# The layer boundary of a fused eight-layer block: both norms from gathered sums, residual, scaling and split by chunks

## What is computed

```python
def rmsnorm(x, g):
    y = xf * lax.rsqrt(jnp.mean(xf * xf, axis=-1, keepdims=True) + EPS)
    return (y * g.astype(jnp.float32)).astype(x.dtype)

def modulated_sublayer(x, mod, g_pre, g_post, fn, weight):
    shift, scale, gate = mod[:, 0], mod[:, 1], mod[:, 2]
    h = rmsnorm(x, g_pre) * (1.0 + scale) + shift
    y = rmsnorm(fn(h), g_post)
    return x + weight * (1.0 + gate) * y
```

## Time and profile before

| | |
|---|---|
| time, median of 3 runs | 3411.46 us (3410.39 to 3413.81) |
| the profiled execution | 3409.45 us, its span 3407.7 us |
| PE busy | 3114.9 us, 91% of the span |
| DVE, ACT, POOL busy | 1680.2, 1172.0, 610.4 us |
| mean granted clock of PE | 0.945 of full speed |

### The profile page before, as it was taken

One profiled execution on the slowest core, in us unless ns is written; L12 is line 12 of the kernel. 1 busy time (PEld: TensorE's weight loads), 2 busy tenths in 40 slices (PEclk: granted clock), 3 DMA queues, 4 the chain that ended last, 5 costly groups with the idle time before them and its releaser, 6 DMA issues.

```text
span 3407.7 us, 39522 instructions
## 1 busy us (share of the span) xinstructions
PE 3114.9 (91%) x13788; PEld 2440.5 (72%) x13788; DVE 1680.2 (49%) x2588; ACT 1172.0 (34%) x2027; POOL 610.4 (18%) x359
## 2 busy tenths in 40 slices
PE   5999968999899997588899997997899999969999
PEld 3888846888678885376588885775777767757777
DVE  5554466554554335786411104375566424745663
ACT  3222233222232222365322223444444334344442
POOL 0000000000000000101243442113211331132113
PEclk7999979999999998799899998898899998989999
DMA  4555513555343332100123332112111220121112
GB/s 188 195 174 169 172 53 119 174 181 167 123 136 124 98 96 69 41 13 28 66 91 94 99 102 66 50 38 87 56 44 38 81 73 31 50 75 62 40 42 80
DMA packets 88154, 313.92 MB, mean 92 GB/s; under 512 B 10208, under 2 KB 11104, under 8 KB 87904
## 3 DMA queue, kind: packets, MB, share of 16 engines
q1 hardware_dynamic: 64848, 233.59, 21.3%
q0 software_dynamic: 19488, 71.31, 6.2%
q10 hardware_dynamic: 3696, 7.38, 0.7%
HBM read 308.05 MB, written 2.10 MB: 91 GB/s over the span
## 4 chain that ended last, share of the span: by engine, by line
PE 43%; issue 42%; POOL 9%; DVE 3%; DMA 1%; ACT 1%; POOLq 0%; SPq 0%; DVEq 0%; ACTq 0%
PE psum L365 36%; POOL w_lo L350 9%; PE psum L1886 3%; PE psum L881 1%; PE psum L558 1%; DVE rstd L441 1%; PE psum L851 1%; DMA ada_first<-ada_in 1%; DVE ada_acc L544 1%; PE psum L1830 0%; DVE X L521 0%; DVE ta L515 0%; DVE tb L477 0%; DMA raw<-stream_in 0%; PE psum L1832 0%
## 5 line engine op out<-in xcount | busy, mean ns | idle before, releaser
L350 POOL TENSOR_TENSOR w_lo<-raw,w_hi 128x1024 fp32r<-128x1024 f32 x225 | 540.8, 2410 | 1807.5 <-ACT w_hi L321 1612.5
L365 PE MATMUL psum<-h_hi,w_hi 128*128 128x512 f32 x1824 | 497.2, 406 | 44.5 <-DVE h_lo L489 31.6
L365 PE MATMUL psum<-h_hi,w_lo 128*128 128x512 f32 x1824 | 484.8, 399 | 0.0
L365 PE MATMUL psum<-h_lo,w_hi 128*128 128x512 f32 x1824 | 484.2, 399 | 0.0
L365 PEld LDWEIGHTS psum<-h_hi,w_hi 128*128 128x128 f32 x1824 | 349.3, 192 | 139.3 <-issue 56.6
L365 PEld LDWEIGHTS psum<-h_hi,w_lo 128*128 128x128 f32 x1824 | 347.0, 190 | 83.8
L365 PEld LDWEIGHTS psum<-h_lo,w_hi 128*128 128x128 f32 x1824 | 346.6, 190 | 84.4
L335 ACT ACTIVATE w_hi<-raw 128x1024 fp32r<-128x1024 f32 x256 | 257.2, 1046 | 144.3 <-DMA raw<-stream_in 144.3
L341 DVE TENSOR_TENSOR w_lo<-raw,w_hi 128x1024 fp32r<-128x1024 f32 x192 | 227.8, 1223 | 107.7 <-ACT w_hi L335 101.2
L688 DVE TENSOR_TENSOR tb<-ta,psum 128x512 f32<-128x512 f32 x88 | 60.3, 686 | 404.2 <-PE psum L365 352.0
L642 ACT ACTIVATE a_hi<-tb 128x512 f32 (+1 forms) x88 | 55.6, 632 | 557.6 <-DVE tb L688 557.6
(11 more groups left out here) (370 smaller groups left out, 4690.4 us busy)
## 6 DMA issues: line engine op xcount, KB each, us to landing
raw<-stream_in SPq DMA_DIRECT2D x433, 512.0 KB, 3.5
ada_raw<-ada_in POOLq DMA_DIRECT2D x128, 512.0 KB, 4.7
ada_first<-ada_in POOLq DMA_DIRECT2D x2, 2048.0 KB, 20.9
ada_first<-ada_in SPq DMA_DIRECT2D x2, 2048.0 KB, 24.4
X<-xT_in ACTq DMA_DIRECT2D x1, 2048.0 KB, 8.8
out_x<-X SPq DMA_DIRECT2D x8, 256.0 KB, 2.9
qt_hi<-qr_hi ACTq DMA_DIRECT2D x16, 64.0 KB, 2.0
qt_lo<-qr_lo ACTq DMA_DIRECT2D x16, 64.0 KB, 2.0
```

Source lines behind the costliest of these rows:

```text
L350: pool.tensor_tensor(w_lo[:, u % RING], raw[:, u % RAW], w_hi[:, u % RING].bitcast(F32), ALU.subtract).then_inc(lo_ready, 1)
L365: mm = pe.matmul(dst, w[wi], m[mi], start=(first and n == 0), stop=(last and n == total - 1), skip_group_check=skip)
```

## The change

The norm over y and the norm over the new X are both worked out from three sums per token: of y squared, of z squared and of X times z, where z is y times its column of gains and gate (so that the mean square of the new X is that of the old one, plus two terms). These are gathered while the last products of the layer are still running. Both squares come from ACT, the product X times z from DVE, and the running sums over chunks 0 to 6 from DVE. After the last product, PE adds over partitions with the gathered tile as the weights and one column of ones as the moving side (`column_sums`, four matmuls of one column), so root and reciprocal work on 128x4 values. PE then spreads such a 128x4 tile to 128x512 in PSUM by four matmuls against an identity (`spread_pe`).

In the pool layer the squares are not gathered on DVE: PE makes their column sums for each chunk (`post_chunk_pe`), behind the products of the next chunk.

After the two spreads DVE works through the chunks with three operations each (`move`, `scale_dve`, `low_dve`); the residual add of chunk 0 is DVE's, those of chunks 1 to 7 GpSimd's (`post_gpsimd`). `dense_first` now takes four units: three side by side, the fourth four chunks behind. The splits of units 2 and 3 of the next layer move into the boundary, those after them to behind it. The table load for Silu, and the DMAs of constants in mla and hy 0, move to behind the eight chunks on ACT. The loops over the halves of the down product are written out. ffn0 and hy 1, which have no such boundary before them, sum the squares of X by `column_sums` and spread the result.

```diff
+        def column_sums(pe, squares, b, column, first=False):
+            for t in range(4):
+                mm = pe.matmul(psum[:, b, column + t:column + t + 1], squares[:, t * P:(t + 1) * P], ones[:, 0:1],
+                               start=(first and t == 0), stop=True, skip_group_check=True)
+        def spread_pe(pe, label, row, b):
+            pe.wait_ge(inverses.sem, inverses.at(label))
+            for t in range(4):
+                mm = pe.matmul(psum[:, b, t * P:(t + 1) * P], stat[:, row, t:t + 1].broadcast_to((P, P)),
+                               ident[:], start=(t == 0), stop=(t == 3), skip_group_check=True)
+        def post_chunk_dve(dve, own_order, L, n, g, y):
...
+                op = dve.tensor_scalar(y[:, n], bank(g + n), bcol[:, n:n + 1], None, ALU.mult)
+            product = dve.scalar_tensor_tensor(out=rstd[:] if n == 0 else tb[:, 1], in0=X[:, n], scalar=2.0 / D,
+                                               in1=y[:, n], op0=ALU.mult, op1=ALU.mult)
...
+                added = dve.tensor_tensor(rstd[:], rstd[:], tb[:, 1], ALU.add)
+                if L != "pool":
+                    own_order.link(dve.tensor_tensor(std[:], std[:], sq[:, 0], ALU.add))
+                    added = dve.tensor_tensor(tb[:, 0], tb[:, 0], sq[:, 1], ALU.add)
+        def post_pe(pe, L):
...
+                pe.wait_ge(gathered.sem, chunks + NC - 1)
+                column_sums(pe, std[:], 4, 0, first=True)
+                column_sums(pe, rstd[:], 7, 4, first=True)
+                column_sums(pe, tb[:, 0], 7, 8)
+            pe.wait_ge(sq_ready.sem, squares + 2 * NC - 1)
+            sums.give(column_sums(pe, last_y, 4, 0), (F, "y"))
+            pe.wait_ge(gathered.sem, chunks + NC)
+            column_sums(pe, tb[:, 1], 7, 4)
+            pe.wait_ge(sq_ready.sem, squares + 2 * NC)
+            sums.give(column_sums(pe, last_z, 7, 8), (F, "z"))
+            spread_pe(pe, (F, "r"), 2, 6)
+            spread_pe(pe, (F, "s"), 5, 5)
+        def post_chunk_pe(pe, L, n):
+            pe.wait_ge(sq_ready.sem, sq_ready.at(F) + 2 * n + 2)
+            tile = (sq, ta)[n % 2]
+            column_sums(pe, tile[:, 0], 4, 0, first=(n == 0))
+            sums.give(column_sums(pe, tile[:, 1], 7, 8, first=(n == 0)), (F, n))
+        def post_dve(dve, own_order, L, y, after, columns, shift, ahead):
...
+            def move(c):
+                moved.give(dve.tensor_tensor(ta[:, c % 2], y[:, c], psum[:, 6], ALU.mult), (L, c))
+            move(0)
+            for c in range(NC):
+                if c + 1 < NC:
+                    if c == 1:
+                        dve.wait_ge(x_ready.sem, x_ready.at((L, 0)))
+                    elif c >= 2:
+                        dve.wait_ge(added.sem, added.at((L, c - 1)))
+                    move(c + 1)
+                if c == 0:
+                    dve.wait_ge(moved.sem, moved.at((L, 0)))
+                    x_ready.give(dve.tensor_tensor(X[:, 0], X[:, 0], ta[:, 0], ALU.add), (L, 0))
+                    dve.wait_ge(spread.sem, spread.at((F, "s")))
...
+                else:
+                    low_dve(dve, after, c - 1, shift)
+                    dve.wait_ge(added.sem, added.at((L, c)))
+                scale_dve(dve, after, c, columns)
+                if ahead is not None and c in (1, 3):
+                    split_lo(dve, ahead + c // 2)
+            low_dve(dve, after, NC - 1, shift)
+        def post_gpsimd(pool, L):
+            for c in range(1, NC):
+                if c < 3 and ahead(L) is not None and ahead(L) >= own["by_gpsimd"]:
+                    low_gpsimd(pool, ahead(L) + c - 1)
+                pool.wait_ge(moved.sem, moved.at((L, c)))
+                added.give(pool.tensor_tensor(X[:, c], X[:, c], ta[:, c % 2], ALU.add), (L, c))
-        def dense_first(pe, L, u, g):
+        def dense_first(pe, L, u, g, units, lag=4):
+            for k in range(NC + lag):
...
+                for m in range(units):
+                    c = k if m < 3 else k - lag
```

More of the change, by code:

```diff
@@ L241, in plan_norm, with plan_pre @@
             rstd_ready.plan(L)
[L243 to L256, removed]
-                for c in range(NC):
-                    scaled.plan((L, c))
-                    part_hi.plan((L, c))
-                    h_ready.plan((L, c))
-        def plan_post(L):
+        FULL = ("ffn0", ("hy", 1))
+        def plan_pre(L):
+            if L in FULL:
+                for c in range(NC):
+                    sq_ready.plan((L, "pre", c))
+                    sums.plan((L, "pre", c))
+                for signal in (roots, inverses, spread):
+                    signal.plan((L, "pre"))
+            for c in range(NC):
+                scaled.plan((L, c))
+                part_hi.plan((L, c))
+                h_ready.plan((L, c))
+        def plan_post(L):
+            F = (L, "post")
+            sq_ready.plan_loop(F, 2 * NC)
+            gathered.plan_loop(F, NC)
+            if L == "pool":
+                sums.plan(*[(F, n) for n in range(NC - 1)])
+            sums.plan((F, "y"), (F, "z"))
+            means.plan(F)
+            for which in ("r", "s"):
+                for signal in (roots, inverses, spread):
+                    signal.plan((F, which))
+            x_ready.plan((L, 0))
             for c in range(NC):
-                x_ready.plan((L, c))
+                moved.plan((L, c))
+            for c in range(1, NC):
+                added.plan((L, c))
         def plan_ffn(L):
@@ L342, in split_lo_loop, with low_gpsimd, lows_gpsimd @@
                               ALU.subtract).then_inc(lo_ready, 1)
[L344 to L358, removed]
+        def low_gpsimd(pool, u, i=None):
+            pool.wait_ge(hi_ready, u + 1 if i is None else i * RING + (u + 1))
+            pool.tensor_tensor(w_lo[:, u % RING], raw[:, u % RAW], w_hi[:, u % RING].bitcast(F32),
+                               ALU.subtract).then_inc(lo_ready, 1)
+        def lows_gpsimd(pool, first, end):
+            rounds = (end - first) // RING
+            if rounds:
+                with pool.Fori(0, rounds) as i:
+                    for k in range(RING):
+                        low_gpsimd(pool, first + k, i)
+            for u in range(first + rounds * RING, end):
+                low_gpsimd(pool, u)
         def three_passes(pe, dst, weights, moving, first=True, last=True, skip=False):
@@ L442, in norm_dve @@
             dve.wait_ge(rstd_ready.sem, rstd_ready.at(L))
[L444 to L462, removed]
@@ new lines, in column_dve, with pre_dve @@
+        def column_dve(dve, own_order, to, gains, index, weight=1.0):
+            dve.wait_ge(mod_ready, index + 1)
+            own_order.step(dve.scalar_tensor_tensor(out=to[:], in0=mod[:, index], scalar=1.0, in1=gains,
+                                                    op0=ALU.add, op1=ALU.mult))
+            if weight != 1.0:
+                own_order.step(dve.tensor_scalar(to[:], to[:], weight, None, ALU.mult))
+        def pre_dve(dve, L, columns, shift=None):
+            dve.wait_ge(spread.sem, spread.at((L, "pre")))
+            scale_dve(dve, L, 0, columns)
+            for c in range(NC):
+                if c + 1 < NC:
+                    scale_dve(dve, L, c + 1, columns)
+                low_dve(dve, L, c, shift)
@@ L602, in ffn_pe @@
             pe.wait_ge(evac.sem, evac.at(("g", g1 - 7)))
-            with pe.Fori(0, 2) as i:
+            for i in range(2):
                 for n in range(4):
@@ L1283, in mla_act @@
             u, g = u + 4, g + 4
-            for k in range(2, 5):
+            for k in range(1, 5):
                 split_hi(act, u + k)
```

504 lines of the change are left out of this document (295 added, 209 removed).

## The result

The changed kernel takes 3370.55 us (median of 4 runs, 3368.13 to 3373.75), the kernel before beside it 3412.64 (3410.39 to 3416.49): ratio 0.9876, 95% interval 0.9859 to 0.9893, 42 us faster. The forecast was 3398 within 3348 to 3413, and 3386 to 3411 for the likeliest case alone. The direction held, and the time lies inside the wide range; the size was off by a factor of three, and the cause forecast for it turned out to be worth almost nothing.

What follows compares the result with a forecast made beforehand. TensorE was taken to bound the kernel nearly throughout, losing time in seven boundaries (185 us), a DVE chain. Gains 7 + 10 + 10 + 8 - 1 - 21 - 4 + 3 = 12, with rounding 13: 3398 us, range 3348 to 3413.

Steps and rivals of the forecast that it cites:

- the likeliest case: Whole kernel: the main forecast, 3398 us, with its own range of 3386 to 3411 and a chance of 0.50.
- 24 matmuls of 0.234 follow the last chunk: Boundaries: dense products after the last chunk of h, in the 27.1 us from first product to end of four units.
- the written-out loops: Down product: writing out the loops gains nothing, since PE has no gap in loops now.
- the gathering under the products: DVE's added gathering, 2.8 us per group, lies under the products; without that cover it would cost 2.1 us a group.
- 0.87 a matmul, so 3.5 us a spread: Boundaries: price of spreading by four 128-column matmuls, taken between bounds of 0.45 and 1.7 us a matmul.
- eight times four column sums are 3.7 warm and 7.2 slow: Start of hy 1: column sums there instead of 7.6; with the 3.5 spread replacing most of the reciprocal, gain -4.
- 20 to 21 us: Boundaries: seven chunk periods of 3.2 us, the last without adds, two with a split of 1.22 in two boundaries.
- The splits in the boundary are covered likewise: Boundaries: the moved weight splits are covered; the fifth unit's late split ends about 3.4 us before PE wants it.
- The block: Boundary chunks: GpSimd's add holds SBUF and DVE's h_lo waits each time, so 3.2 us a chunk instead of 2.4.
- The clock: PE taken at 1.2 GHz (0.50) in the boundaries' spreads and the pool layer, whose rounds become 5.8 us; pool gain -21.
- the two rivals with a warm clock or without a block: Clock holds through column sums: 3351, chance 0.17; GpSimd does not block DVE: 3380, chance 0.13.
- The slow start: Rival: chunk-paced products do not wake PE's clock, some 13 us a boundary, 65 in five, 3463; chance 0.11.

Runs made afterwards that it cites:

- a32: The changed kernel with 32 unused bytes ahead of ones and h_hi, so tiles lie 32 past a multiple of 64 bytes as before the change: 3411.18 us, ratio 0.9998.
- a128: The changed kernel with the tile small laid over stat, so ones, h_hi and all behind begin at a multiple of 128 bytes: 3352.02 us, ratio 0.9833.
- b32: The kernel before with 32 unused bytes ahead of ones and h_hi, so these begin at a multiple of 128 bytes: 3350.86 us, ratio 0.9817.
- b96: The kernel before with 96 unused bytes ahead of ones and h_hi, giving the changed kernel's remainder, 64 past a multiple of 128: 3374.64 us, ratio 0.9905.
- a_evac: The changed kernel with ACT in both hybrid layers copying a product out of PSUM before making the next weight split: 3357.70 us, ratio 0.9852.
- a_mla: The changed kernel with ACT's splits of units 4 and 5 of mla ahead of the norm of the latents: 3368.23 us, ratio 0.9872.
- a_dveadd: The changed kernel with all eight residual adds on DVE, GpSimd keeping its splits: 3356.99 us, ratio 0.9845.
- b_w32: The kernel before with 32 unused bytes ahead of w_hi: weights 32 past a multiple of 128 bytes, h at one: 3411.12 us, ratio 0.9999.

## Why the prediction was right, and where it failed

**What failed: the pace of the dense stream.** Every term carried 0.233 to 0.234 us a matmul over from before ("24 matmuls of 0.234 follow the last chunk"), and I charged the written-out loops with nothing. The loops were right, and so was the gathering under the products: with the placement of before, the rests of the four ffn layers take the same 1416.3 us (a32). But the change also moved every tile behind `small` by 608 bytes, which the diff says in two lines that I didn't cost. Some 8,800 dense matmuls of 512 columns at full clock went from 0.2334 to 0.2290, 39 us; a32 against the changed kernel says 41. That is nearly the whole measured gain of 42. That the time still lies between 3348 and 3413 is luck: none of the cases behind that range had this term, and without it the kernel stands at 3411 (a32).

**What was mis-sized: the boundaries.** With that taken out, the change proper was forecast at 13 and is -1 (a128 against b32) to 4 (the changed kernel against b96), which the intervals don't tell from nothing. Its two sides were both larger than I had them. In a32, which has the placement of before, the stretches around the boundaries gain 25 against my 12: the sum of 0.4, 3.2, -16.8, 42.2 and -3.6. The step was the price of a spread, "0.87 a matmul, so 3.5 us a spread": it is 3.5 to 3.93 us for both, so 0.44 to 0.49 a matmul, the lower bound that I had (one column at 1.2 GHz) and not the value near the middle. That takes some 3 us off each of the six boundaries with two spreads, but only in the one to ffn2 did the first product come so much earlier: 15.0 us after the last one, 17.6 forecast. To mla it is 15.6 for 16.4; to ffn3 and hy 0 it is 15.4 and 15.7 where I had about 15.1 and 15.4, because I let the clock fall later there. It did not: from the start of the column sums to the first spread it takes 7.1 and 7.4 us there, as in the boundary to ffn2 (7.4). The longer first block (`h_lo` 2.32, where I had 1.75) took 0.6 of it wherever GpSimd also makes a split.

The start of hy 1 has a slip of mine: "eight times four column sums are 3.7 warm and 7.2 slow". They are 32 matmuls, and by the row behind my price (eight in 1.84 or 3.58) that makes 7.4 and 14.3. They took:

```profile
2691.91 9.27 PE L468 MATMUL psum<-ones,sq 128*128 128x1 f32 x64
```

The single spread behind them took 2.08 and not 3.5; altogether this boundary lost 1.7 us and not 4. In ffn0 the same sums took 13.8 us, and its start gained 1.1 instead of 3. And, by my own numbers, "20 to 21 us" for seven periods plus 24 matmuls of 0.234 make 25.6 to 26.6, not the 27.1 that I went on with; measured are 26.7 to 27.0.

**What was missing: the layers behind.** "The splits in the boundary are covered likewise" looked only at the boundary. The splits that moved there moved the later ones too. In the hybrid layers these now stand ahead of copies that PE waits for, and in mla one of GpSimd's runs beside `cq_lo`. a_evac and a_mla give back 13 and 2 to 4 us. Against b96 the changed kernel is 20 us longer in the rests of mla, hy 0 and hy 1 (285.1, 637.9 and 636.1 against 280.5, 625.2 and 633.2); so about 15 of the 20 are these two places. In a32 those rests lose 31: in its profile the hybrid layers' rests are 8 and 10 us longer than in the changed kernel, where placement explains some 4 each (before against b96: 3.8 and 3.6). PE idles there as long in both kernels (45 to 47 us), but the granted clock is at 0.50 for 96 and 89 us in a32 and for 82 and 72 in the changed kernel. Why this is so stays open; that execution was also 4 us above the median of its kernel.

**What was right.** The block: GpSimd first, DVE's `h_lo` waiting each time, period 3.2 (measured 3.18), add 1.23 (measured 1.27 to 1.29 where nothing holds it). The Trainium skill (SBUF — State Buffer, Who interferes with whom) says that a VectorE instruction with two SBUF inputs contends with a GpSimd instruction that reads SBUF, and a_dveadd agrees with it: with no such add `h_lo` is back at 0.75. The estimate of 1.36 from the Trainium skill (GPSIMD Engine Reference, Elementwise — side-by-side cycle accounting) was 0.08 too long, my half of the 1024-column row 0.05 too short. The clock: 0.50 from the fourth group of column sums on, in the spreads, and through the pool layer's output chunks, rounds of 5.8 forecast and 5.55 measured; the two rivals with a warm clock or without a block, 3351 and 3380, are out, though their times lay nearer to the result. The end of four units in the four boundaries: 44.7, 43.6, 42.2 and 44.5 forecast, 41.7, 42.3, 42.3 and 42.7 measured. The slow start did not keep the clock down, as the windows from the first product of mla on show:

```profile
1316.60:1320.80 4.20, 4.15 (x10) 3.28 (x11) 4.01 (x5) 1.08 (x2) 2.41 (x2) 0.50 0.42 125
1320.80:1343.00 22.20, 20.41 (x86) 15.68 (x85) 15.74 (x18) 5.25 (x8) 5.15 (x4) 0.99 0.08 28
```

## What to carry to other kernels

Before a gain is put down to a change, compare the pace of a stretch that the change doesn't touch; here nearly the whole gain lay in that pace. A new tile in SBUF is an edit of its own: look at where it pushes the operands of the hottest matmul, and try the old kernel with a few unused bytes first. And where work is moved forward in a ring, follow what is queued behind it in the layers that come later: 20 of the 23 us that the boundaries won over b96 were lost again there.

## What was not expected of the hardware

- The pace of back-to-back fp32r matmuls of 512 columns at clock 1.00 depends on how the streaming tile and the weight tile lie to each other: 0.2268 us with equal remainders by 128 bytes (0 and 0, 64 and 64), 0.2290 with the streaming tile 64 ahead of the weights, 0.2334 with it 96 ahead, or 32 short (96 and 0, 0 and 32). It isn't symmetric: in the changed kernel the 96 products with w streaming at 0 and h as weights at 64 start 0.2333 apart (PE's timeline below: 39 pairs in 18.20 us). So the difference of the two remainders by 128 doesn't sort all rows. By 256 it does: there the streaming tile is ahead of the weights by 0 in all kernels with 0.2268, by 64 in those with 0.2290 (byte 93632 against 41088), and by 32, 96, 160, 192 or 224 where it is 0.233 to 0.234. No run has it ahead by 128, and none says why; so the unit stays open. The Trainium skill (TensorE: Matmul & The Clock Gate, Step-by-step: what each phase is for) says that weight loads have a read port of their own and take nothing from the running matmul; b_w32 against b32, where of these matmuls' tiles only the weights lie elsewhere, shows 60 us that this doesn't explain.

```profile
2083.11 0.63 PE L382 MATMUL psum<-w_hi,h_hi 128*128 128x512 f32 x2
...
2101.31 0.63 PE L382 MATMUL psum<-w_hi,h_hi 128*128 128x512 f32 x2
```

- At 1.2 GHz a plain fp32 matmul of 128 columns costs hardly more than one of a single column: eight in 3.93 us against eight in 3.55.
- PE busy 45.00 of 45.00 us, with weight loads all along, stays at 0.50; the matmuls there have 1 to 144 columns.
